# Second mixture-of-experts layer: token rows picked and summed by TensorE instead of gathered and scattered through HBM

## The reference

```python
def routed_experts(h, expert_idx, expert_w, w_gate, w_up, w_down):
    ...
    def run_block(args):
        tok, wt, e = args
        xb = h[tok]
        hid = jax.nn.silu(xb @ w_gate[e]) * (xb @ w_up[e])
        return (hid @ w_down[e]) * wt[:, None]
    ...
    return jax.ops.segment_sum(y.reshape(n_slots, d), slot_tok, num_segments=n_tok)
...
x_l = x_l + gate_l * rms_norm(y[n_c:].reshape(b, S, d), g_post)
```

## Time and profile before

| | us |
|---|---|
| median of 3 runs | 2045.66 |
| lowest and highest of them | 2041.65, 2048.55 |
| profiled execution | 2038.08 |
| its span, first to last instruction | 2036.3 |
| busy in it: PE, DVE, ACT, POOL | 1608.0, 898.2, 574.4, 347.3 |
| mean granted TensorE clock | 0.918 |
| data moved | 578.28 MB, mean 284 GB/s |

### The profile page before, as it was taken

The page is one execution under the profiler, slowest core; times in us unless marked ns, Lnnn a source line. Parts: engine busy times, 40 slices in busy tenths (PEclk is TensorE's granted clock), DMA queues, the critical chain, the costliest instruction groups (busy, mean ns, idle before and its releaser), DMA issues. The chain is left out here.

```text
span 2036.3 us, 39515 instructions
## 1 busy us (share of the span) xinstructions
PE 1608.0 (79%) x11503; PEld 697.9 (34%) x11504; DVE 898.2 (44%) x3018; ACT 574.4 (28%) x1197; POOL 347.3 (17%) x357
## 2 busy tenths in 40 slices
PE   3999689868989899888896499867767666766685
PEld 2544554422333333323332365544322222221221
DVE  2154683444444444444455426553533332322334
ACT  2142372222332333323332215143112221211222
POOL 0002300012222222222220001030121111211220
PEclk8999899999999999999998789978888887878998
DMA  8313710467999989998847743624699999999974
GB/s 280 135 70 134 281 64 1 186 234 289 388 405 413 391 348 406 413 358 346 342 156 309 245 152 124 250 105 155 238 410 403 413 401 413 412 405 380 409 308 188
DMA packets 165603, 578.28 MB, mean 284 GB/s; under 512 B 24956, under 2 KB 29792, under 8 KB 148648
## 3 DMA queue, kind: packets, MB, share of 16 engines
q1 hardware_dynamic: 134592, 515.49, 64.7%
q0 software_dynamic: 24256, 60.03, 7.9%
q10 hardware_dynamic: 6696, 1.98, 0.4%
HBM read 557.87 MB, written 37.89 MB: 293 GB/s over the span
## 5 line engine op out<-in xcount | busy, mean ns | idle before, releaser
L1254 PE MATMUL bank<-arena 128*32 128x512 f32 x4160 | 539.1, 638 | 167.4 <-DMA arena<-in_exp_w_up 139.6
L1279 PE MATMUL bank<-arena 128*32 128x512 f32 x2048 | 249.3, 600 | 68.2 <-issue 67.7
L699 POOL DMA_INDIRECT yrows<-arena x128 | 130.1, 1016 | 858.3 <-ACT arena L941 858.3
L1254 PEld LDWEIGHTS bank<-arena 128*32 128x32 f32 x4160 | 125.4, 114 | 355.6 <-issue 327.3
L935 ACT ACTIVATE arena<-bank 128x128 f32<-128x128 f32 x128 | 35.6, 278 | 629.5 <-PE bank L1313 629.5
L1777 DVE TENSOR_TENSOR arena<-arena,bank 64x512 f32<-64x512 f32 x130 | 88.4, 680 | 258.6 <-ACT arena L919 258.6
L680 POOL DMA_INDIRECT arena<-hrows,arena x134 | 137.2, 1024 | 132.5 <-DVE arena L1765 91.9
L1749 DVE COPY arena<-arena 128x12 bf16 (+1 forms) x272 | 60.5, 223 | 188.9 <-issue 188.9
L1012 PE MATMUL bank<-arena 128*128 128x512 f32 (+3 forms) x384 | 132.4, 507 | 11.7 <-DVE arena L1433 11.7
L941 ACT ACTIVATE arena<-bank 128x512 f32<-128x512 f32 x128 | 76.5, 597 | 166.8 <-PE bank L1279 166.8
L1279 PEld LDWEIGHTS bank<-arena 128*32 128x32 f32 x2048 | 60.3, 109 | 163.4 <-issue 161.7
(11 more groups left out here) (305 smaller groups left out, 1856.7 us busy)
## 6 DMA issues: line engine op xcount, KB each, us to landing
arena<-in_exp_w_gate SPq DMA_DIRECT2D x128, 1024.0 KB
arena<-in_exp_w_up SPq DMA_DIRECT2D x128, 1024.0 KB
arena<-in_exp_w_down SPq DMA_DIRECT2D x128, 1024.0 KB
arena<-in_w_ada SPq DMA_DIRECT2D x10, 3072.0 KB, 12.0
arena<-yrows SPq DMA_DIRECT2D x24, 1024.0 KB, 16.3
arena<-in_w_ada SPq DMA_DIRECT2D x8, 2048.0 KB, 12.7
arena<-in_w_in SPq DMA_DIRECT2D x8, 2048.0 KB, 13.4
arena<-in_w_out SPq DMA_DIRECT2D x4, 2048.0 KB, 9.9
```

Of the source, the lines that this page charges most:

```text
L699: pool.indirect_dma_start(out=yrows, out_offset=bass.IndirectOffsetOnAxis(ap=SIXS[u], axis=0), in_=YSB[u], in_offset=None, bounds_check=2 ...
L1254: ins = pe.matmul(bank[0][r:r + UNIT, :], XGT[:, c, un, hh, :], wv[un][:, :, hh, c, :], start=(c == 0), stop=(c == 3))
L1279: ins = pe.matmul(bank[2][r:r + UNIT, :], HIDT[:, c, UNIT * un:UNIT * un + UNIT], wv[un][:, c, cg * 512:(cg + 1) * 512], start=(c == 0), s ...
```

## The change

**Second layer's routed experts.** No token row passes through HBM. The modulated tokens stay on chip (`HM`). Per block, PE multiplies a float32 one-hot matrix `OHF` (tokens against 64 slots) twice: with `KVPW` (per token its number and its weight for the unit's expert) for the list, into `bank[5]`, and with `HM` for the token rows, into `bank[4]` (`pick_and_gather`); ACT copies the rows to `XG[0]` (`xg`), and the turn goes on as before. DVE keeps token number and weight of each slot in `SLOTW` (`slot_rows`) and builds from them `OHW`, slots against tokens with the weight as value (`weighted`). PE multiplies `OHW` with the block's results `YSB[0]` and adds into four banks that stay open through the whole loop (`combine`); the shared expert's down product goes into these banks first, and the copy of it to `YS` is gone. The combine in iteration `b` is that of block `b - 1`; it stands between the turn of the tokens and the down product. The pick stands at the head of the iteration, ahead of the up product. Behind the loop one last combine closes the banks, and the normalization reads them directly, in halves of 512 columns, each stored on its own. `hrows`, `yrows`, `WK`, `DG` and the reads back are used in the first layer only.

**First layer.** The order of the 128 half rows in `XG` and `YSB` is another (64 first halves, then 64 second halves), the one-hot `OH` is half as wide, and `rows` has one operation more.

**Start.** The first three loads of `w_ada` are issued by SP ahead of the first barrier, on semaphores that this barrier doesn't clear; `c` and `c_ctx` are loaded first; in the first layer PE multiplies piece 0 ahead of the turns of the tokens.

The diff, cut to its core:

```diff
@@ start
+                sp.dma_start(HC[:, 0, :], I["c_ctx"].rearrange("(p c) -> p c", c=8)).then_inc(sp_first[0], 16)
+                sp.dma_start(HC[:, 1, :], I["c"][0].rearrange("(p c) -> p c", c=8)).then_inc(sp_first[0], 16)
...
+                w_ada = lay("w_ada", 0).rearrange("(p c) n -> p c n", c=8)
+                for n in range(3):
+                    sp.dma_start(at(ring[n], 8, 512), w_ada[:, :, n * 512:(n + 1) * 512]).then_inc(sp_land[n], 16)
+                sp.wait_ge(sp_first[2], 64)
...
-        nc.all_engine_barrier(sems_to_clear=all_sems)
+        nc.all_engine_barrier(sems_to_clear=sems_behind_first)
@@ scalar
+                def xg(val):
+                    act.wait_ge(pe_gx, val)
+                    if not (isinstance(val, int) and val == 1):
+                        act.wait_ge(pe_x, val - 1)
+                    act.activation(XG[0], bank[4][:, :], ACT.Copy).then_inc(a_xg, 1)
...
                 with act.Fori(0, pairs) as i:
                     for u in range(2):
+                        if last:
+                            xg(i * 2 + (u + 3))
...
+                        if last:
+                            act.wait_ge(pe_cmb, i * 2 + (u + 1))
+                        else:
+                            act.wait_ge(pool_s[u], i * 16 + 16)
@@ tensor
+                if l == 0:
+                    ada_piece(0, 0, 512)
                 transposes(0, (0, 1, 2, 3))
...
+                def pick_and_gather(n):
+                    pe.wait_ge(v_oh, n)
+                    for i in range(2):
+                        for h in range(2):
+                            ins = pe.matmul(META[SLOTS * h:SLOTS * h + SLOTS], OHF[:, i, :], KVPW[:, i, :], start=(i == 0), stop=(i == 1))
+                    ins.then_inc(pe_meta, 1)
+                    for i in range(2):
+                        for h in range(2):
+                            ins = pe.matmul(bank[4][SLOTS * h:SLOTS * h + SLOTS, :], OHF[:, i, :], HM[:, i, h * 512:(h + 1) * 512],
+                                            start=(i == 0), stop=(i == 1))
+                    ins.then_inc(pe_gx, 1)
...
+                def combine():
+                    for i in range(2):
+                        for cg in range(2):
+                            r = slice(SLOTS * cg, SLOTS * cg + SLOTS)
+                            ins = pe.matmul(bank[acc[i][cg]][:, :], OHW[r, i, :], YSB[0][r, :], start=False, stop=False)
+                    return ins
...
                 with pe.Fori(0, blocks) as b:
                     word = pe.snap(word_next)
                     e, slot, step = experts_of(word)
                     pe.wait_ge(a_xe, b + 2)
+                    if last:
+                        pick_and_gather(b + 3)
                     pe.wait_ge(v_gu, b + 1)
...
+                    if last:
+                        turn_tokens(0, b + 3)
...
                     pe.reg_mov(word_next, experts_word(b + 2))
+                    if last:
+                        pe.wait_ge(a_y, b + 2)
+                        pe.wait_ge(v_ow, b + 1)
+                        combine().then_inc(pe_cmb, 1)
                     pe.wait_ge(a_h, b + 1)
                     pe.wait_ge(a_y, b + 2)
...
                     in_slots(slot_now, step_now, down_now)
-                    meta(b + 5, b + 4)
+                    if not last:
+                        meta(b + 5, b + 4)
@@ vector
+                def weighted(b, chain):
+                    dve.wait_ge(v_ix, b + 1)
+                    chain(dve.tensor_copy(S2, SLOTW[:, :, bass.ds(b, 1)].rearrange("p a n -> p (a n)")))
+                    dve.wait_ge(pe_cmb, b + 1)
+                    dve.tensor_scalar(OHW.rearrange("p i n -> p (i n)"), IOTA2.rearrange("p i n -> p (i n)"), S2[:, 0:1], S2[:, 1:2],
+                                      ALU.is_equal, ALU.mult).then_inc(v_ow, 1)
...
+                        if last:
+                            dve.wait_ge(pe_meta, b + 3)
+                            slot_rows(b + 2, chain)
+                            dve.wait_ge(pe_gx, b + 3)
+                            one_hot(b + 3, chain)
```

456 lines of the change are left out of this document (285 added, 171 removed).

## The result

The change takes the kernel from a median of 2043.66 us (2041.44 to 2048.55) to **1975.14 us** (1970.31 to 1976.27): ratio 0.9657, 95% interval 0.9631 to 0.9683, so 3.4% faster. The profiled execution of after took 1974.16 us, its span 1972.17.

A forecast was written before the change was run, and what follows sets the result against it. The second layer's loop, bound by bytes, was to become TensorE-bound at 11.5 us a block. Loop +23 us, tail -23.7 and start -4 gave -4.7: forecast 2041 us as median, range 2012 to 2078.

The forecast's parts named there:

- Bytes: Second layer's expert loop: after the change 189 MB at 404 GB/s take 468 us, 9.7 us per block.
- Pick, list, combining: TensorE work added per block of the second layer's loop: pick 1.85 us, list +0.25, combine 1.9.
- The base: Second layer's loop: TensorE's existing work per block, 7.5 us, taken from the first layer's 7.6 us.
- Holes, "I take zero": Second layer's loop: combine may cover up to 0.4 us of idle time, a second break may cost as much; net zero.
- Rival 1: Second layer's loop: combine covers the hole ahead of down, picks take 1.7 us; 11.0 us per block, 2018 us; chance 27%.
- The three microseconds of stalls on weights: Second layer's loop: runs of one-unit experts can stall on weight loads; 3 us allowed for all of them.
- The tail: From the second layer's last down product to the end: direct reading of the banks gains 23.7 us (21 to 25).
- The start: Kernel start: modulation loads issued ahead of the barrier gain at most the idle 4.3 us; -4 us (-6 to +2).
- the +2 at the end of the range: Kernel start: slow end of the early loads' range, a loss of 2 us against the expected -4.
- The first layer, zero: First layer: same TensorE counts, half-wide one-hot, list one operation longer; no change, +-4 us.
- The head of the second layer: Ahead of the second layer's first up product: sixteen WK steps on DVE go, about 1 us won.
- the forecast of -4.7: Whole kernel: sum of +23 us, -23.7 and -4, taking the profiled run from 2038.1 to 2033.4 us.

## Why the prediction was wrong, step by step

- **Bytes**: 404 GB/s and 9.7 us a block (468 us) were forecast; with the combining gone the loop sits at 488. TensorE is the bound in after, as forecast, but the DMA share is not 0.85: it is 0.93 over the loop, since the loop got shorter than thought.

```profile
1450.00:1950.00 500.00, 500.00 (x3660) 165.97 (x3656) 145.36 (x560) 144.46 (x281) 0.00 (x0) 1.00 0.93 373
```

- **Pick, list, combining**: right to 0.1 us. Pick and list take 2.10 us from start to start; 2.21 were in the sum (1.85 + 0.25, and 0.11 for the old list, which takes 0.22 from start to start with all eight instructions). The combining takes 1.92 (1.9). The side by side running, taken from the earlier trace rows, was shown by taking it away: 3.70. The Trainium skill (TensorEngine Tiling (Array Packing), Key Properties) says that a change of tiling mode drains the array. After's loop, with one more such change, has no idle time in 100 us; the eight instructions of the combining fill 1.92 us, where four pairs at the 0.43 us of the earlier trace rows are 1.72, so all that a border costs is at most 0.2, and it was in the forecast's number.
- **The base**: this is the step that failed. 7.5 us was the mean block of the first layer, said to be bound by nothing but TensorE. But TensorE was busy there 90.38 of 100 us only the earlier trace rows, so 0.73 us of each 7.6 were holes, and the same row gives 6.87 without them. One block of that stretch in before, 7.37 us from up to up:

```profile
764.89 2.78 PE L1254 MATMUL bank<-arena 128*32 128x512 f32 x24 [0.35 <-issue]
768.98 0.75 PE L1244 MATMUL bank<-arena 128*128 128x128 f32 x4
770.19 1.92 PE L1279 MATMUL bank<-arena 128*32 128x512 f32 x16 [0.46 <-issue]
772.04 0.29 PE L1237 MATMUL bank<-arena 128*64 128x3 bf16 x8
772.26 2.78 PE L1254 MATMUL bank<-arena 128*32 128x512 f32 x24
```

  In after's loop the same pieces (up, hidden turn, token turn, down) take 6.62 us from start to start, where 7.39 stood in the sum. That is 0.77 less. Together with the 0.11 of pick and list and the 0.02 of the combining it makes the 0.86 between 11.5 and 10.64, times 48 blocks 41 us of the miss of 44 in this loop.
- **Holes, "I take zero"**: the holes were kept in the base while new queued work stood in front of them. Rival 1 had the mechanism, and the sum with it came to 11.0 because it allowed 0.4 us for the one hole. Over the whole first loop of before the hole ahead of down was 0.68 on the mean and the one ahead of up 0.2. Of the first, 0.25 is what is left where copies are prompt. That this part is the sequencer's branching behind a wait is shown from both sides: the combining behind the branches brings holes of 0.19 on the mean into the new loop, and the branches ahead of the wait take 0.25 down to 0.09 in the first layer. Some 0.4 is the late copy, which isn't in this loop any more. Its cause is open, and so is what it was about the old loop that brought it. That the pick covers the hole ahead of up was only argued. "Nothing shows that work queued ahead of a branch covers it" was true, and a reason to try rival 1's sum with the full holes, not to leave them in.
- **The three microseconds of stalls on weights**: after has none, but the second block takes 14.7 us, 4 more than the period.
- **The tail**: right, 24.2 for 23.7, by its own terms (11.7 us to VectorE's end for 11.9).
- **The start**: right in kind, too small. "At most the idle 4.3 us" failed: the fourth load lands 5.6 us earlier (33.90 for 39.54). And less work stands behind it: the project product follows 9.9 us later and not 11.6. The early issues cost the barrier 2.3 us (ScalarE's first work behind it begins at 14.46 for 12.20), for which there was slack. No row shows where the +2 at the end of the range comes from; no run shows such a loss. 7.3 us at the first project product, 8.6 at the first up product; as a kernel of its own the edit is worth 7 us.
- **The first layer, zero**: right for the kernel, wrong for this pair of traces. With that layer's changes and the start alone the kernel is no faster than with the start alone. The 14.7 us go with the late copies, which in the groups at 2045 are in 76 of 80 blocks in before and in 33 in after. In the groups at 2021, where no copy is late, the loop takes 620.3 us with the old code and 617 to 621 with after's. That is no experiment on the late copy itself, whose cause is open.
- **The head of the second layer**: 1 us of gain forecast, 3.3 lost. 2.2 of them are there before the first list burst (373.2 us behind the last down product for 371.0), and arise ahead of the new work, and 1.1 between that burst and the first up product (10.6 for 9.5). Other kernels with the new second layer lose 0 to 6 us here. The cause is open.

Over all, of the 59 us between the forecast of -4.7 and the -64.1: 44 are the second layer's loop, 37 of it the base, 15 the first layer's loop, 5 the start, less 4 for the head. The miss would be 15 us smaller without the late copies of those groups, but the time would still lie below the range. (The forecast's own loop sum is 2019.2 and not 2019.5, which changes nothing.)

## What to carry to other kernels

Before you take a measured block as TensorE's time, take its idle time out: list the instructions from start to start and see whether the sum is the period. In this kernel the hole ahead of a product behind a wait and a chain of branches was covered by independent products queued ahead of the wait (0.19 us a block), and it shrank when the wait was put inside the branch (0.25 to 0.09 us), which is worth only what the next bound leaves of it. And compare two traces only beside the kernel before in the same group of runs: of 24 us of apparent gain between two spans, 17 were the group's.

## What the runs showed of the hardware that was not expected

- Two 64-row halves of the array overlap across the order of issue: four instructions of one half and then four of the other take 1.99 us as when they alternate by twos, and 3.70 when all eight are on one half.
- In some groups of runs ScalarE's copy started up to 1.7 us behind the product that releases it and not 0.48, in a loop where GpSimd issues real gathers; in before in 76 of 80 blocks, in after in 33 of 40 odd ones. An empty gather (0.09 us behind the turn) and a real one in another loop, in groups of that kind, left the copy at 0.48. The cause is open.
- The same program is 1.0 to 1.4% apart between two kinds of group (2021 to 2023 and 2042 to 2049 us). Most of it seems to lie in one loop: 639.5 us in the trace of before, 620.3 in the one of its loop's code from the other kind of group. Whether it is the chip isn't known.
